# A two-layer hybrid block: RMS root applied after the up projection, attention chains spread over more weight units, convolution taps on GpSimd

## The chip, the cores and the metric

The kernel runs on one core of a Trainium2 chip. The metric is the device time of one execution in microseconds. The kernel before takes 2891.14 us (median of three runs, 2889.9 to 2891.33). The span is the part of an execution that the profile records.

## The reference, cut to what matters

Two transformer-like layers on 256 tokens of width 2048, all float32. What the change touches:

```python
# layer 1
h = rmsnorm(x, g_mix) @ w_in
z, xbc, dt, q, k, v, qi, ki, wi = _split(h, IN_SIZES)
xbc = silu(causal_dwconv(xbc, conv_w, conv_b))          # 4 taps, 1536 channels
y = ssd_chunked(...)                                     # Mamba-2 mixer
y = (y + d_skip * xs) * silu(z)
y_ssd = groupwise_rmsnorm(y, 2 groups) * g_ssd
y_att = dsa_attention(q, k, v, qi, ki, wi)               # 8 heads, top-64 keys
x = x + concat([y_ssd, y_att]) @ w_out
u = rmsnorm(x, g_mlp) @ w_up                             # 2048 -> 8192
x = x + square(relu(u)) @ w_down                         # 8192 -> 2048
# layer 2
proj = rms_norm(x, ln1_w) @ w_in
o_a = nsa_attention(nsa_q, nsa_kv, nsa_gate, ...)
qkv = silu(causal_depthwise_conv(gdn_qkv, conv_w))       # 4 taps, 3072 channels
o_b = gated_deltanet(qkv, gdn_z, ...)
x = x + (g_a * (o_a @ w_pa) + g_b * (o_b @ w_pb)) @ w_o
h = rms_norm(x, ln2_w)
x = x + square(relu(h @ w_up)) @ w_down
```

rmsnorm divides each token's row by its root mean square and multiplies each channel by a gain. Since the divisor is one number per token, `rmsnorm(x, g) @ w` equals `((x*g) @ w) / root`, token by token.

## The kernel before, in words

Activations lie transposed: 128 channels on the partitions, 256 tokens along the free dimension; such a 128x256 piece is a tile, two side by side are a pair. Every big product is float32-exact by splitting: `hi` is the value rounded to the fast type fp32r, `lo` the rest, and TensorE adds hi·hi, hi·lo and lo·hi. So weights and activations both exist as hi and lo.

Weights stream from HBM by SyncE into a ring of four 1 MB pieces (`ring`). Half a piece is a unit (128x1024, eight k-tiles). For each unit ScalarE casts `w_hi` (L1732) and VectorE subtracts `w_lo` (L1036); four such units are held, and ScalarE casts unit n+4 only when TensorE has used unit n. `split_to(unit + UNITS)` issues these two in each engine's program. A column of an output tile takes two units where k is 2048, and TensorE calls L441 (hi weights against hi and lo activations, 512 wide) and L444 (lo weights, 256 wide).

The order of the work is written out by hand. Each engine has its own program made of Python generators. `drain(a, b, project(...))` advances all of them in turn, one step each, and calls that a round; one round holds one weight unit of the projection. `rounds(n)` in a side chain lets n units pass before its next step. The number of rounds must be matched between the engines' programs, since an engine takes its instructions strictly in order: what waits on a semaphore holds all that is behind it.

The places that the change touches:

- `attention(c)`, two chains c = 0 and 1 of three steps sets each, run beside the 24 units of the xbc projection: TensorE logits (L614), VectorE mask, maximum, reciprocal, scale (L1230 to L1237), ScalarE exponentials (L1897), TensorE transposes (L622), ScalarE copy, TensorE output (L633). Both chains do each step in the same round.
- `conv` (L1249 to L1269) evacuates an xbc or GDN tile on VectorE and then computes the four taps there: one L1259 or L1262 and three L1265 per tile, 12 tiles of xbc and 24 of GDN, in all 144 instructions. ScalarE's silu (L1916) of tile t-1 follows after it has lifted tile t.
- `ssd_prepare`, `ssd_output`, `ssd_gate` are the Mamba mixer, beside the z projection and the attention half of the output projection. `ssd_gate` squares the gated output per group (L1969), TensorE sums it over the partitions with a matrix of ones (L705), ScalarE takes the root (L1972), VectorE scales. Group 1 follows group 0 with the same buffers and bank.
- `gathered_norm`, `norm`, `column_pair` start an MLP. The squares of x are taken during the product before (`project_gathered`, L1799, added on GpSimd, L2275); then TensorE sums them (L522 to L526), ScalarE takes the root (L1782), VectorE the reciprocal (L1088), and for each of eight pairs VectorE multiplies by gain and root (L1095), ScalarE casts `h_hi` (L1786), VectorE subtracts `h_lo` (L1099). `column_pair` (L435, L436) computes two output tiles together and waits for each pair of h.
- In the MLP itself `up_tile` and `squared_relu` bring a tile of u from the bank (L1738 and L1056 are the lift and the add of the two halves), then max(u,0)·u in one instruction (L1369), ScalarE's cast (L1995) and VectorE's rest (L1372).

## Time and profile before

| | us |
|---|---|
| median of three runs | 2891.14 |
| the profiled execution, its own time | 2889.39 |
| its span | 2887.2 |
| TensorE busy | 2743.2 (95%) |
| VectorE busy | 1869.5 (65%) |
| ScalarE busy | 1311.0 (45%) |
| GpSimd busy | 35.5 (1%) |

The stages in the order of time, in us from the span's start, as the instructions' lines place them in the timeline: attention chains and xbc from 208 to 305, mixer and z from 308, the output projection until 478, first MLP norm until 505, first MLP body until about 1209, the first half of GDN projections with NSA attention from about 1372 to 1485, the second half with the delta rule from about 1541 to 1648, second MLP norm from 2145 to 2170, second MLP body until 2868. In the MLP bodies TensorE is busy without a gap; its idle time lies between them.

### The profile page before, as it was taken

The numbers are of one execution on the slowest core, as the hardware profiler recorded it, in microseconds if no ns is written. First come the engines' busy times: TensorE is split into PE (matmuls) and PEld (weight loads), VectorE is DVE, ScalarE is ACT, GpSimd is POOL, SyncE is SP. The second block draws the span as 40 slices with busy tenths as digits, with TensorE's granted clock in tenths as the row PEclk, the third lists the DMA queues.
The fourth block names the chain that finished last, engine by engine and source line by source line (L and its number), as shares of the span: only waits on it lengthen the run. The fifth ranks groups of instructions, "written<-read, shape, count | busy, mean of one in ns | idle before, by whom it ended". The sixth has DMA issues, their size and how long they took to land. (4 is left out here: it accounts for less than half of the span.)

```text
span 2887.2 us, 38158 instructions
## 1 busy us (share of the span) xinstructions
PE 2743.2 (95%) x15614; PEld 2366.2 (82%) x15614; DVE 1869.5 (65%) x2582; ACT 1311.0 (45%) x1805; POOL 35.5 (1%) x36
## 2 busy tenths in 40 slices
PE   7998998999999999999898989999989999999998
PEld 6777877888888888788676868878878888888887
DVE  5687687666656666665667767666666666566665
ACT  4545544434434344355554444444434444343443
POOL 0000001000000000100000000000000000000000
PEclk9999999999999999999999999999999999999999
DMA  5344434555555555556232323345445555555553
GB/s 215 134 178 140 152 132 146 190 195 185 192 187 191 190 188 190 208 190 231 102 105 90 122 81 117 132 169 184 173 161 185 189 187 189 186 187 192 188 191 116
DMA packets 66422, 482.05 MB, mean 167 GB/s; under 512 B 7400, under 2 KB 7528, under 8 KB 9033
## 3 DMA queue, kind: packets, MB, share of 16 engines
q1 hardware_dynamic: 64944, 468.74, 46.9%
q0 software_dynamic: 928, 9.70, 0.9%
q8 instruction: 124, 2.03, 0.3%
q10 hardware_dynamic: 376, 1.17, 0.1%
q14 instruction: 50, 0.40, 0.0%
HBM read 473.30 MB, written 6.29 MB: 166 GB/s over the span
## 5 line engine op out<-in xcount | busy, mean ns | idle before, releaser
L1036 DVE TENSOR_TENSOR w_lo<-weight_ring,w_hi 128x1024 fp32r<-128x1024 f32 x886 | 1079.8, 1231 | 592.7 <-ACT w_hi L1732 590.8
L441 PE MATMUL bank<-h,w_hi 128*128 128x512 f32 x4144 | 1333.4, 403 | 4.3 <-DVE h L1702 4.3
L1732 ACT CAST w_hi<-weight_ring 128x1024 fp32r<-128x1024 f32 x886 | 916.7, 1048 | 619.7 <-PE bank L444 602.1
L444 PEld LDWEIGHTS bank<-h,w_lo 128*128 128x128 f32 x4144 | 786.4, 190 | 186.6
L444 PE MATMUL bank<-h,w_lo 128*128 128x256 f32 x4144 | 822.0, 280 | 0.0
L441 PE MATMUL bank<-mix,w_hi 128*128 128x512 f32 x2560 | 808.3, 397 | 6.6 <-DVE w_lo L1036 6.6
L441 PEld LDWEIGHTS bank<-h,w_hi 128*128 128x128 f32 x4144 | 641.7, 191 | 23.3 <-issue 20.0
L444 PEld LDWEIGHTS bank<-mix,w_lo 128*128 128x128 f32 x2560 | 481.9, 188 | 113.8
L444 PE MATMUL bank<-mix,w_lo 128*128 128x256 f32 x2560 | 504.0, 278 | 0.0
L441 PEld LDWEIGHTS bank<-mix,w_hi 128*128 128x128 f32 x2560 | 391.3, 189 | 8.1 <-issue 7.8
L1738 ACT COPY arena<-bank 128x256 f32<-128x256 f32 x283 | 104.6, 371 | 393.4 <-PE bank L444 390.8
L1056 DVE TENSOR_TENSOR arena<-arena,bank 128x256 f32<-128x256 f32 x281 | 117.8, 420 | 161.1 <-ACT arena L1738 160.6
L1106 DVE TENSOR_TENSOR arena<-arena,bank 128x256 f32<-128x256 f32 x176 | 73.9, 420 | 63.2 <-PE bank L444 63.1
L435 PE MATMUL bank<-h,w_hi 128*128 128x512 f32 x128 | 56.4, 468 | 32.8 <-DVE h L1099 32.8
L1109 DVE TENSOR_TENSOR arena<-arena,bank 128x256 f32<-128x256 f32 x176 | 74.1, 421 | 6.0
L1995 ACT CAST mix<-arena 128x512 fp32r<-128x512 f32 x64 | 39.7, 620 | 82.9 <-DVE arena L1369 82.9
L1372 DVE TENSOR_TENSOR mix<-arena,mix 128x512 fp32r<-128x512 f32 x64 | 44.4, 693 | 43.9 <-ACT mix L1995 43.9
L435 PEld LDWEIGHTS bank<-h,w_hi 128*128 128x128 f32 x128 | 28.4, 222 | 46.0 <-DVE h L1099 22.3
L1799 ACT ACTIVATE arena<-arena 128x512 f32<-128x512 f32 x32 | 20.2, 632 | 95.6 <-DVE arena L1109 72.6
L1265 DVE SCALAR_TENSOR_TENSOR arena<-arena,vecs 128x255 f32<-128x255 f32 (+2 forms) x108 | 52.2, 483 | 3.9
L2275 POOL TENSOR_TENSOR arena<-arena 128x512 f32<-128x512 f32 x24 | 31.2, 1302 | 1839.2 <-ACT arena L1799 1839.2
L1369 DVE SCALAR_TENSOR_TENSOR arena<-arena 128x512 f32<-128x512 f32 x64 | 44.3, 692 | 6.7
(318 smaller groups left out, 1496.9 us busy)
## 6 DMA issues: line engine op xcount, KB each, us to landing
weight_ring<-in_w_up SPq DMA_DIRECT2D x128, 1024.0 KB, 4.9
weight_ring<-in_w_down SPq DMA_DIRECT2D x128, 1024.0 KB, 4.9
weight_ring<-in_w_merge SPq DMA_DIRECT2D x32, 1024.0 KB, 4.8
weight_ring<-in_w_gdn SPq DMA_DIRECT2D x24, 1024.0 KB, 4.9
weight_ring<-in_w_papb SPq DMA_DIRECT2D x16, 1024.0 KB, 4.9
...
```

What stands on the lines that cost most here:

```text
L435: e.matmul(bank[:, :], hi, x[:, :, at:at + S], start=first, stop=False)
L441: e.matmul(bank[:, :], w_hi[:, unit_at % UNITS, o + j * P:o + (j + 1) * P], x[:, :, at + j * S:at + (j + 1) * S], start=first and j == 0, ...
L444: done = e.matmul(bank[:, 0:S], w_lo[:, unit_at % UNITS, o + j * P:o + (j + 1) * P], x[:, 0, at + j * S:at + (j + 1) * S], start=False, st ...
L1036: e.tensor_tensor(w_lo[:, i, :], ring[:, p % PIECES, half * UNIT:(half + 1) * UNIT], w_hi[:, i, :].bitcast(F32), ALU.subtract).then_inc(un ...
L1056: e.tensor_tensor(dst, dst, bank[:, 0:S], ALU.add).then_inc(read, 1)
L1106: e.tensor_tensor(tile(xT, t), tile(xT, t), bank[:, 0:S], ALU.add).then_inc(res_half, 1)
L1109: e.tensor_tensor(tile(xT, t), tile(xT, t), bank[:, S:2 * S], ALU.add).then_inc(read, 1)
L1265: e.scalar_tensor_tensor(out=a[:, back:S], in0=src[:, 0:S - back], scalar=vec(name, (3 - back) * tiles + t), in1=a[:, back:S], op0=ALU.mul ...
L1369: e.scalar_tensor_tensor(out=buf, in0=buf, scalar=0.0, in1=buf, op0=ALU.max, op1=ALU.mult).then_inc(up_squared, 1)
L1372: e.tensor_tensor(pair(mix_lo, n_up % 8), buf, pair(mix_hi, n_up % 8).bitcast(F32), ALU.subtract).then_inc(up_lo, 1)
L1732: e.copy(w_hi[:, i, :], ring[:, p % PIECES, half * UNIT:(half + 1) * UNIT]).then_inc(unit_hi, 1)
L1738: e.copy(dst, psum[use % 3][0:dst.shape[0], S:2 * S]).then_inc(lifted, 1)
```

## The change

**MLP norms.** The product x·gain, without the root, is now what the MLP multiplies. During the product before (`project_gathered`, `gained_residual`), each finished tile of x is multiplied by the gain, on ScalarE as hi and on VectorE as lo (`gained`). `column_pair` starts on it, `gathered_norm` comes behind it on TensorE, and the root is awaited in the first `relu_scaled`. There max(u,0) is multiplied by 1/root (one VectorE instruction), ScalarE squares, casts, and VectorE's `lo` of a pair is issued one tile later. The first MLP reads `hn` and writes `mix`; the second reads `mix` and writes `hn`. The norms before the first mixer and before layer 2's projections keep their form.

**First mixer.** Chain 1 of the attention starts three rounds after chain 0; the transposes come three rounds behind the logits, and an iteration has six rounds as before. `ssd_prepare` starts three rounds later on all three engines. `ssd_gate` has its own buffers and banks for its two groups, so all four squares come before the first root.

**Convolutions.** VectorE only evacuates the tile. GpSimd computes the taps: a product, then three times a product into a buffer and a sum, seven instructions per tile, each waiting for the one before it, 252 in all. The DMA that brings x back for the residual is behind the 12 xbc tiles in GpSimd's queue.

```diff
@@ -599,6 +602,7 @@
 
             def attention(c):
                 A = ATT
+                yield from rounds(3 * c)
...
@@ -614,7 +618,7 @@
                         done = e.matmul(bank[0][:, j * nk:(j + 1) * nk], tile(qT, h)[:, qb * P:(qb + 1) * P],
                                         tile(kT, h // 2)[:, 0:nk], start=True, stop=True)
                     done.then_inc(att_pe[c], 1)
-                    yield from rounds(2)
+                    yield from rounds(3)
...
-                    yield from rounds(2)
+                    yield
 
...
             def ssd_prepare():
                 A = PREP
+                yield from rounds(3)
                 e.wait_ge(conv_silu_done, 12)
...
             def ssd_gate():
+                A = GATE["act"]
+                yield from rounds(2)
                 for g in range(2):
-                    yield
-                    if g == 1:
-                        e.wait_ge(gate_act, GATE["act"]["root"])
                     for j in range(2):
-                        e.wait_ge(gate_act, 5 * g + GATE["act"][f"sq{j}"])
-                        e.matmul(psum[7][:, 0:S], ones[:, :], ysq[j][:, 0:S], start=j == 0, stop=False)
-                        done = e.matmul(psum[7][:, 0:S], ones[:, :], ysq[j][:, S:2 * S], start=False, stop=j == 1)
+                        e.wait_ge(gate_act, A[f"sq{g}{j}"])
+                        e.matmul(psum[6 + g][:, 0:S], ones[:, :], ysq[g][j][:, 0:S], start=j == 0, stop=False)
+                        done = e.matmul(psum[6 + g][:, 0:S], ones[:, :], ysq[g][j][:, S:2 * S], start=False, stop=j == 1)
                     done.then_inc(gate_pe, 1)
                     yield
 
...
+            def mlp(n, x, hid):
+
+                ready = xg_lo, [16 * n + k - k % 2 + 2 for k in range(KD)]
                 for f in range(FF // D):
                     if f == 0:
-                        column_pair(hn, normed(i))
-                        drain(project(KD - 2, hn))
+                        column_pair(x, ready)
+                        gathered_norm(1 + 2 * n)
+                        drain(project(KD - 2, x))
                     else:
-                        drain(project(KD, hn))
-                    drain(project(KD, mix, 0, KD, (up_lo, [8 * (4 * n + f) + k // 2 + 1 for k in range(KD)])))
-
-            mlp(1)
+                        drain(project(KD, x))
+                    drain(project(KD, hid, 0, KD, (up_lo, [8 * (4 * n + f) + k // 2 + 1 for k in range(KD)])))
+
+            mlp(0, hn, mix)
...
                 V, A = ATT["dve"], ATT["act"]
                 pr, st = relu_buf[c], (st0, st1)[c]
+                yield from rounds(3 * c + 1)
                 e.wait_ge(score_added, 4 * QI_T)
...
                     e.tensor_reduce(st[:, 0:nh], split(pr, nh), AX_X, ALU.max, negate=True).then_inc(att_dve[c], 1)
+                    yield
                     e.wait_ge(att_act[c], 3 * it + A["exp"])
...
+            n_xg = 0
+
+            def gained(t, gain, dst):
+
+                nonlocal n_xg
+                e.wait_ge(xg_hi, n_xg + 1)
+                e.scalar_tensor_tensor(out=tile(dst[:, 1, :], t), in0=tile(xT, t), scalar=vec(gain, t),
+                                       in1=tile(dst[:, 0, :], t).bitcast(F32), op0=ALU.mult,
+                                       op1=ALU.subtract).then_inc(xg_lo, 1)
+                n_xg += 1
+
+            def gained_residual(gain, dst):
+                def evacuate(t, bank, read):
+                    residual(t, bank, read)
+                    if t > 0:
+                        gained(t - 1, gain, dst)
+                    if t == KD - 1:
+                        gained(t, gain, dst)
                 return evacuate
 
-            drain(attention(0), attention(1), project(12, 2, conv(xbcT, "conv_w", XBC_T, conv_acc_1, 0, "conv_b")))
+            drain(attention(0), attention(1), project(12, 2, to_tiles(xbcT)))
...
+                    if n_up % 32 == 0:
+                        e.wait_ge(norm_root, 2 + 2 * (n_up // 32))
+                        e.reciprocal(root_m, root_m).then_inc(norm_rstd, 1)
+                        e.wait_ge(norm_rstd, 2 + 2 * (n_up // 32))
+                    e.scalar_tensor_tensor(out=split(buf, 2), in0=split(buf, 2), scalar=0.0, in1=over(root_m, 2), op0=ALU.max,
+                                           op1=ALU.mult).then_inc(up_scaled, 1)
                     n_up += 1
                 use += 1
 
+            def up_tiles(first, hid):
                 nonlocal unit
-                for t in range(n):
+                for t in range(first, KD):
                     for i in range(2):
                         split_to(unit + UNITS)
                         unit += 1
                         if i == 1:
-                            squared_relu(t)
+                            relu_scaled(t)
+                            if t % 2 == 0 and t > 0:
+                                squared_lo(n_up - 1, hid)
+                            elif t == KD - 1:
+                                squared_lo(n_up - 1, hid)
                         yield
 
             def mlp(...):
-                split_to(unit + UNITS)
-                norm(i, gain, sq_m, root_m, root_m)
...
+            def project_gathered(per_use, gain=None, dst=None):
+
                 nonlocal unit, use, n_gathered
+
+                def finish(t, at_use):
+                    bank_done(e, at_use)
+                    if gain:
+                        e.activation(tile(dst[:, 0, :], t), tile(xT, t), ACT.Copy, scale=vec(gain, t)).then_inc(xg_hi, 1)
+                    if t % 2:
+                        gather(t // 2, at_use)
+
                 for t in range(KD):
                     for i in range(per_use):
                         split_to(unit + UNITS)
                         unit += 1
                         if i == per_use - 1:
-                            if t % 2:
-                                bank_done(e, use - 1)
-                                gather(t // 2, use)
+                            if t > 0:
+                                finish(t - 1, use - 1)
+                            if t == KD - 1:
+                                finish(t, use)
                             use += 1
                         yield
                 n_gathered += 1
...
-                    e.wait_ge(conv_taps, 4 * (n_conv + 1))
+                    e.wait_ge(conv_taps, 7 * (n_conv + 1))
...
+                    if n_up % 32 == 0:
+                        e.wait_ge(norm_summed, 9 + 2 * (n_up // 32))
+                        e.activation(root_m, psum[7][:, 0:S], ACT.Sqrt, bias=eps[:, 0:1], scale=1.0 / D).then_inc(norm_root, 1)
+                    e.wait_ge(up_scaled, n_up + 1)
+                    e.activation(buf, buf, ACT.Square).then_inc(up_squared, 1)
                     e.wait_ge(up_squared, n_up + 1)
-                    e.copy(pair(mix_hi, n_up % 8), buf).then_inc(up_hi, 1)
+                    e.copy(pair(hid[:, 0, :], n_up % 8), buf).then_inc(up_hi, 1)
...
+            def conv(stage, dst, name, tiles, acc, t_buf, first, with_bias=None):
+
+                nonlocal n_conv, n_tap
+                for i in range(12):
+                    t, src, a = first + i, tile(dst, i), acc[:, (i % 2) * S:(i % 2 + 1) * S]
+                    bank_done(e, USE[stage] + i)
+                    if n_conv >= 2:
+                        e.wait_ge(conv_silu_done, n_conv - 1)
+                    if with_bias:
+                        e.tensor_scalar(a, src, vec(name, 3 * tiles + t), vec(with_bias, t), ALU.mult,
+                                        ALU.add).then_inc(conv_taps, 1)
+                    else:
+                        e.tensor_scalar(a, src, vec(name, 3 * tiles + t), None, ALU.mult).then_inc(conv_taps, 1)
+                    n_tap += 1
+                    for back in (1, 2, 3):
+                        e.wait_ge(conv_taps, n_tap)
+                        e.tensor_scalar(t_buf[:, back:S], src[:, 0:S - back], vec(name, (3 - back) * tiles + t), None,
+                                        ALU.mult).then_inc(conv_taps, 1)
+                        e.wait_ge(conv_taps, n_tap + 1)
+                        e.tensor_tensor(a[:, back:S], a[:, back:S], t_buf[:, back:S], ALU.add).then_inc(conv_taps, 1)
+                        n_tap += 2
+                    n_conv += 1
+
             e.wait_ge(rows_copied, NSA_HEADS)
             e.dma_start(bias_rows, rows).then_inc(rows_written, 16)
+            e.wait_ge(vecs_loaded, 16)
+            conv("xbc", xbcT, "conv_w", XBC_T, conv_acc_1, sq0, 0, "conv_b")
...
+            for half in range(2):
+                conv(f"gdn{half}", gdn_in[half], "conv_w2", 24, conv_acc_g[half], (sqc, arena[:, 1536:2048])[half],
+                     12 * half)
```

Three places show how the instructions move. The first is VectorE in the first GDN half, where an NSA iteration meets a projected tile. Before, from the tile's evacuation (L1056) through chain 0's into chain 1's softmax (L1541 to L1552):

```order
L1056 TENSOR_TENSOR arena<-arena,bank 128x256
L1262 TENSOR_SCALAR arena<-arena,vecs 128x256
L1265 SCALAR_TENSOR_TENSOR arena<-arena,vecs 128x255
L1265 SCALAR_TENSOR_TENSOR arena<-arena,vecs 128x254
L1265 SCALAR_TENSOR_TENSOR arena<-arena,vecs 128x253
L1541 SCALAR_TENSOR_TENSOR arena<-bank,arena 128x256
L1545 TENSOR_REDUCE arena<-arena 128x2
L1547 RECIPROCAL arena<-arena 128x2
L1549 TENSOR_TENSOR arena<-arena 128x2
L1552 TENSOR_TENSOR arena<-arena 128x256
L1541 SCALAR_TENSOR_TENSOR arena<-bank,arena 128x256
```

Now (L1060 is the evacuation, L1553 to L1564 the softmax):

```order
L1060 TENSOR_TENSOR arena<-arena,bank 128x256
L1553 SCALAR_TENSOR_TENSOR arena<-bank,arena 128x256
L1557 TENSOR_REDUCE arena<-arena 128x2
L1559 RECIPROCAL arena<-arena 128x2
L1561 TENSOR_TENSOR arena<-arena 128x2
L1564 TENSOR_TENSOR arena<-arena 128x256
L1553 SCALAR_TENSOR_TENSOR arena<-bank,arena 128x256
```

The four tap instructions between the evacuation and the softmax are gone from VectorE.

The second is VectorE at the start of the attention chains, behind the end of the top-k selection (L1194, L1196). Before, chain 0 (L1230 to L1237), chain 1, then two weight units (L1036) and the first conv tile:

```order
L1194 TENSOR_SCALAR arena<-arena 128x256
L1196 TENSOR_TENSOR arena<-arena,const_mats 128x128
L1230 SCALAR_TENSOR_TENSOR arena<-bank,arena 128x512
L1233 TENSOR_REDUCE arena<-arena 128x4
L1235 RECIPROCAL arena<-arena 128x4
L1237 TENSOR_TENSOR arena<-arena 128x512
L1230 SCALAR_TENSOR_TENSOR arena<-bank,arena 128x512
L1233 TENSOR_REDUCE arena<-arena 128x4
L1235 RECIPROCAL arena<-arena 128x4
L1237 TENSOR_TENSOR arena<-arena 128x512
L1036 TENSOR_TENSOR w_lo<-weight_ring,w_hi 128x1024 x2
L1056 TENSOR_TENSOR arena<-arena,bank 128x256
```

Now (L1235 to L1243 is chain 0, L1040 a weight unit, L1060 an evacuated tile, L1198 and L1200 the selection's end):

```order
L1040 TENSOR_TENSOR w_lo<-weight_ring,w_hi 128x1024
L1235 SCALAR_TENSOR_TENSOR arena<-bank,arena 128x512
L1238 TENSOR_REDUCE arena<-arena 128x4
L1040 TENSOR_TENSOR w_lo<-weight_ring,w_hi 128x1024
L1060 TENSOR_TENSOR arena<-arena,bank 128x256
L1241 RECIPROCAL arena<-arena 128x4
L1243 TENSOR_TENSOR arena<-arena 128x512
L1040 TENSOR_TENSOR w_lo<-weight_ring,w_hi 128x1024 x2
L1060 TENSOR_TENSOR arena<-arena,bank 128x256
L1235 SCALAR_TENSOR_TENSOR arena<-bank,arena 128x512
```

A unit and an evacuation now stand between chain 0's maximum and its reciprocal, and chain 1 comes behind two more units instead of in front of them.

The third is TensorE at the start of the second MLP. Before, the last w_o products, the sums of squares (L522 to L526), then the column pair on h:

```order
L441 MATMUL bank<-h,w_hi 128x512 x2
L444 MATMUL bank<-h,w_lo 128x256 x2
L522 MATMUL bank<-arena,ones 128x256
L523 MATMUL bank<-arena,ones 128x256
L525 MATMUL bank<-arena,ones 128x256
L526 MATMUL bank<-arena,ones 128x256
L435 MATMUL bank<-h,w_hi 128x512
L436 MATMUL bank<-h,w_lo 128x256
L435 MATMUL bank<-h,w_hi 128x512
```

Now the last products of the column pair (L438, L439, 64 rows of them straight behind the w_o products), the sums (L525 to L529), then the next column:

```order
L438 MATMUL bank<-mix,w_hi 128x512
L439 MATMUL bank<-mix,w_lo 128x256
L438 MATMUL bank<-mix,w_hi 128x512
L439 MATMUL bank<-mix,w_lo 128x256
L525 MATMUL bank<-arena,ones 128x256
L526 MATMUL bank<-arena,ones 128x256
L528 MATMUL bank<-arena,ones 128x256
L529 MATMUL bank<-arena,ones 128x256
L444 MATMUL bank<-mix,w_hi 128x512 x2
```

The sums moved from in front of the column pair to behind it, and the pair reads `mix`, not a normed h.

## Rows read from the trace of the kernel before

**Rows 1.** the page, part 1: busy time and share of the span by engine

```profile
PE 2743.2 (95%) x15614; PEld 2366.2 (82%) x15614; DVE 1869.5 (65%) x2582; ACT 1311.0 (45%) x1805; POOL 35.5 (1%) x36
```

**Rows 2.** TensorE's waits over the span: total us, times, longest us

```profile
PE bank L435 <- DVE h L1099: 32.8, 20, 8.6
...
PE bank L870 <- DVE arena L1552: 11.9, 8, 2.4
PE bank L622 <- DVE arena L1237: 10.6, 4, 3.5
...
PE bank L883 <- DVE arena L1555: 8.1, 5, 1.8
...
PE bank L705 <- ACT arena L1969: 5.4, 2, 4.4
```

**Rows 3.** busy time by stretch: span, us busy (instructions) per engine, granted clock, DMA

```profile
792.00:864.00 72.00, 72.00 (x416) 62.86 (x415) 41.45 (x50) 27.12 (x28) 0.00 (x0) 1.00 0.56 190
...
222.50:308.00 85.50, 76.84 (x436) 67.49 (x436) 67.23 (x108) 47.87 (x82) 0.54 (x1) 0.94 0.49 173
...
1372.00:1490.00 118.00, 98.35 (x549) 83.03 (x548) 81.01 (x168) 63.35 (x130) 0.00 (x0) 0.96 0.30 100
...
1545.00:1655.00 110.00, 99.64 (x629) 89.01 (x628) 87.55 (x164) 47.66 (x83) 0.00 (x0) 0.95 0.33 115
```

**Rows 4.** timeline at the two MLP norms: start us, us, instruction, idle before

```profile
478.42 0.60 PE L522 MATMUL bank<-arena,ones 128*128 128x256 f32 x2
...
505.07 0.70 PE L441 MATMUL bank<-h,w_hi 128*128 128x512 f32 x2
...
2144.73 0.59 PE L522 MATMUL bank<-arena,ones 128*128 128x256 f32 x2
...
2147.47 1.28 ACT L1782 ACT_TABLE_LOAD   x1
...
2149.27 1.75 DVE L1088 RECIPROCAL arena<-arena 128x256 f32<-128x256 f32 x1 [0.56 <-ACT arena L1782]
...
2170.13 0.70 PE L441 MATMUL bank<-h,w_hi 128*128 128x512 f32 x2
```

**Rows 5.** timeline of the attention chains and the mixer's start

```profile
219.51 1.11 PE L622 MATMUL bank<-const_mats,arena 128*128 128x128 f32 x4 [3.46 <-DVE arena L1237]
...
308.12 1.12 PE L648 MATMUL bank<-const_mats,arena 128*128 128x128 f32 x4 [3.51 <-ACT arena L1916]
```

**Rows 6.** timeline in the first GDN half's projections

```profile
1392.12 1.52 DVE L1265 SCALAR_TENSOR_TENSOR arena<-arena,vecs 128x255 f32<-128x255 f32 x3
...
1403.90 0.68 PE L883 MATMUL bank<-arena 128*128 128x128 f32 x4 [1.69 <-DVE arena L1555]
...
1484.71 0.42 ACT L1916 ACTIVATE arena<-arena 128x256 f32<-128x256 f32 x1 [1.90 <-DVE arena L1265]
```

**Rows 7.** GpSimd's instructions by line, and a timeline beside VectorE

```profile
L2275 POOL TENSOR_TENSOR arena<-arena 128x512 f32<-128x512 f32 x24 | 31.2, 1302 | 1839.2 <-ACT arena L1799 1839.2
...
L2266 POOL MEMSET ones<- 128x128 f32 x1 | 0.2, 204 | 0.3 <-POOLq L2418 0.3
...
476.31 1.30 POOL L2275 TENSOR_TENSOR arena<-arena 128x512 f32<-128x512 f32 x1 [4.58 <-ACT arena L1799]
...
477.21 1.49 DVE L1036 TENSOR_TENSOR w_lo<-weight_ring,w_hi 128x1024 fp32r<-128x1024 f32 x1 [1.69 <-ACT w_hi L1732]
```

**Rows 8.** the page, part 5: count, busy us and mean ns of one

```profile
L1036 DVE TENSOR_TENSOR w_lo<-weight_ring,w_hi 128x1024 fp32r<-128x1024 f32 x886 | 1079.8, 1231 | 592.7 <-ACT w_hi L1732 590.8
...
L1732 ACT CAST w_hi<-weight_ring 128x1024 fp32r<-128x1024 f32 x886 | 916.7, 1048 | 619.7 <-PE bank L444 602.1
...
L1106 DVE TENSOR_TENSOR arena<-arena,bank 128x256 f32<-128x256 f32 x176 | 73.9, 420 | 63.2 <-PE bank L444 63.1
...
L1799 ACT ACTIVATE arena<-arena 128x512 f32<-128x512 f32 x32 | 20.2, 632 | 95.6 <-DVE arena L1109 72.6
...
L1369 DVE SCALAR_TENSOR_TENSOR arena<-arena 128x512 f32<-128x512 f32 x64 | 44.3, 692 | 6.7
```

158 lines of the change are left out of this document (66 added, 92 removed).

## The prediction

> **What bounds the kernel now.** I read the busy times first. TensorE is busy for 95% of the span [rows 1], so only its idle time and its slow time are to be had: 2887.2 - 2743.2 = 144 us idle. Then the stretches [rows 3]: in an MLP body (792 to 864) it is busy for all 72 us at a granted clock of 1.00, with 416 matmuls, 0.173 us each. A weight unit of 16 matmuls so takes 2.8 us, a column of two units 5.5, a column pair 11.1. In the three other stretches it is idle for 9, 20 and 10 us, and the mean granted clock is 0.94 to 0.96: part of the time it runs at the lower of its levels, 1.2 GHz instead of 2.4. A mean of 0.95 over 100 us costs about 5 us more. The waits then say for whom it waits [rows 2]: VectorE's normed h 32.8 us, the NSA chains 11.9 and 8.1, the attention chains 10.6, the gate's squares 5.4. The timelines show each place [rows 4 to 6].
>
> **The two MLP norms.** From the first sum of squares to the first column behind the pair, 505.07 - 478.42 = 26.65 us pass at the first MLP and 2170.13 - 2144.73 = 25.40 at the second [rows 4]. Of it the pair itself is 11.1 us of work and the four sums about 1.7 (a line of two records shows 0.6). These 12.8 stay. The gain products that replace the norm are ready long before the pair needs the last of them: it asks for tiles 14 and 15 after 14/16 of 11.1 = 9.7 us, and these need two more instructions on VectorE and ScalarE behind the last residual. So 13.8 and 12.6 us go, and what is late next is the root. Behind the pair stand, in order: two lifts on ScalarE (0.9 us), the root with its table load (1.8 from load to reciprocal), the reciprocal 1.75 [rows 4], the scaled relu 0.69, the square 0.63 and a cast of the same size [rows 8]: 6.5 us, and only then ScalarE casts the next weight unit (1.05) and VectorE subtracts (1.23) [rows 8]. That is 8.8 us. TensorE has the sums and two units in hand, 1.7 + 5.6 = 7.3. I charge 1.5 us at the second MLP and 1.1 at the first, where the gate has left the root's table in place. Gain: 12.7 + 11.1 = 23.8 us; the least is 18, if each first root costs 3 us more.
>
> In the MLP bodies 64 squares move to ScalarE, 64 x 0.63 = 40 us, which is busy for 27.1 us of 72 there [rows 3]; I count them at nothing. The last pair's chain to `lo` grows from about 2.8 to 3.8 us, and the down product asks for it 14/16 of a column, 4.9 us, after its start. If that cover of 1.1 us were gone, each of the eight changes from up to down would cost.
>
> The gain products add 16 x 2 instructions in each product before. In the first one a unit takes 2.9 us and VectorE has 1.23 + 2 x 0.42 [rows 8] + about 0.44 = 2.5 us per unit. It fits, with 0.4 to spare.
>
> **Attention chains.** Before, the first transposes waited 3.46 us [rows 5] and all four long ones 10.6 [rows 2]. The stretch loses about 4 us more to the clock. Afterwards chain 0 has three units before its transposes. The first of them still waits: TensorE arrived at 216.05 and will arrive 2.8 us later less half of the logits, near 217.9. VectorE comes from the top-k selection, was done at 219.5 and has one weight unit more in front (1.23), so 220.7. That leaves 2.8 us of wait and about 1.8 of slow clock. The later ones have 8.4 us for a chain of about 4 and go. I take 9 us of gain, between 4 and 13.
>
> **The mixer's start.** It waited 3.51 us for the last silu [rows 5], and then ran slow, some 2.3 us. Three units of cover (8.4 us) replace that. But ScalarE and VectorE both still stand until the last tile's convolution is done, and then have 2.3 us of work for the fourth unit ahead. The limit is a convolution that ends 5.9 us after the tile. I take 1.3 us of stall, a gain of 4.5; between -2 and +6.
>
> **The gate.** 5.4 us of waits for squares go [rows 2]. But VectorE's reciprocals, scalings and rests for both groups now have three units less until the out_ssd column needs them: 2 x (1.75 + 4 x 0.42 + 2 x 0.69) = 9.6 us, with units and residuals of 2.1 between them, against 2.9 per unit on TensorE. I work out a new wait of about 6 us for `lo` of group 1. So nothing is gained, between -4 and +5.
>
> **The convolutions.** VectorE gives up four instructions per tile: 36 tiles, three of them 1.52 us together [rows 6], with the first 1.9. GpSimd's price is not in the trace. Its 512-wide sum takes 1.30 us; a memset of 128 columns 0.20 [rows 7]. For a sum of 255 columns that bounds 0.65 to 1.30, for a product 0.3 to 1.30. I take 0.72 and 0.45, near halved length plus a fixed part: 3 x 0.72 + 4 x 0.45 = 4.0, and six waits of 0.1: 4.6 us per tile. The bounds are 3.2 and 9.1.
>
> VectorE and GpSimd also meet. A w_lo subtraction that started 0.4 us before the end of GpSimd's sum took 1.49 us instead of 1.23 [rows 7, 8]. So each collision costs a wait, on one of the two. Per xbc tile VectorE has two such subtractions, 2.5 us. Were all of it serial, the convolution would take 4.6 + 2.5 = 7.1 us, against a tile every 5.6 in the last five xbc tiles and about 8 to 10 elsewhere.
>
> The Trainium skill speaks against this part: "GPSIMD Engine Reference", § 4.1 Engine selection, advises against elementwise work there, two-input operations at about half VectorE's speed, and "SBUF — State Buffer", § SBUF: two separate sides, says that the shared port pair is an exclusive lock held for a whole instruction. The trace shows the collision, though the subtraction of 1.49 us ended sooner than a lock to the sum's very end would allow (1.63). By such a lock all 2.5 us are serial, towards the first rival. By the first page's 2.6 cycles per element a sum would be about 0.55 us plus its dispatch, and a tile about 4 us, as an estimate.
>
> What it gives: in the first GDN half the wait of 1.69 us at L883 stood behind the taps in VectorE's queue, and the chain in front of L870 began 1.9 us late for the same reason [rows 6, 2]. Both go. The stretch 1372 to 1490 is 20 us idle and loses about 4 by its clock [rows 3]. I leave 3 us of short waits, 3 of collisions and 3.5 at the end, where ScalarE waited 1.90 us for the last taps [rows 6] and will wait about 5. Gain 14.5, between 3 and 22. In the second half (1545 to 1655) 10 us are idle and 5 slow [rows 3], and the delta rule's chains are mostly their own length. Gain 5, between -3 and 10.
>
> **Sum.** 23.8 + 9 + 4.5 + 0 + 14.5 + 5 = 56.8. From the profiled execution's 2889.39 this gives 2832.6. The median is 1.75 us above that execution: 2834.
>
> **The rivals.**
>
> *GpSimd sets the pace in part.* If a tile takes 8 us, which needs each of the seven instructions to wait about 0.5 us for VectorE, the last five xbc tiles fall behind by 4 x 2.4 = 9.7 us and the last silu comes 18.6 us after its tile, 12.7 beyond the limit. The GDN halves give back 7 and 4, as ScalarE is held inside the chains. 24 us less: 2858. For it: VectorE's two-input work fills 2.5 us of each 5.6. Against: GpSimd's own work is half of 8 us.
>
> *VectorE, not TensorE, bounds the output projection.* The gain products come onto an engine that is behind after the gate. If the new wait there is 10 us and the pair starts with VectorE 4 us late, the sum loses 8 to 10: 2843.
>
> *Slower than before.* GpSimd paces all 36 tiles. The three stretches hold them now in about 96 + 118 + 110 = 324 us, 9.0 a tile. With the 24 us from the norms, the sign turns at 348/36 = 9.7 us per tile; at 12 us the kernel takes 2891 + 36 x 12 - 348 = 2975. It needs instructions at their upper bound (9.1 us) and collisions on top. Against it: the memset row.
>
> **How the numbers follow.** The forecast has 0.60, with its own range 2820 to 2848. GpSimd's partial pace 0.20, the output projection 0.12, slower 0.03; 0.05 is left for more gain than I count, to 2815, since the lost time of these stretches is more than what I book. The range that holds it 8 times in 10 is 2818 to 2862. A measurement can tell 0.2%, 6 us, from no change. Faster 0.96, same 0.01, slower 0.03.
>
> **What would show it.** In the profile after: the first MLP column (L435 before) straight behind the product, and 14 to 16 us from the end of the product to the second column, instead of 25 to 27; GpSimd's tile in 4 to 6 us; the waits of the transposes L622 down to one of about 3 us; no wait at L883 for VectorE's copy; a new wait of the out_ssd column for the gate's `lo`. Wrong would be a wait of TensorE for w_lo in the xbc columns, a silu held for more than 6 us, or gaps in the MLP bodies.

## The result and the profile after

The changed kernel takes 2864.04 us, median of 4 runs (2862.56 to 2865.05), against 2891.23 (2889.90 to 2891.82) for the kernel before on the same chip. The ratio is 0.9906 with a 95% interval of 0.9889 to 0.9923. It is faster by 27 us, less than half of the 57 that were forecast, and 2 us outside the range. The profiled execution has a span of 2860.6 us.

Both kernels issue the same 6832 column matmuls by `w_hi` in the same order (L435 and L441 before, L438 and L444 after), so the n-th of them stands for the same piece of work. Start before minus start after is then a gain that can be followed through the program. The table gives what it grows by from one mark to the next. At each mark it is a mean over 17 neighbouring matmuls, because single ones jump where a chain's instructions fall on the other side of them. Before the first mark it is 0.5 us.

| stretch (matmul n, start before) | forecast | measured |
|---|---|---|
| xbc, attention, state preparation and output (8 to 736, to 400.8 us) | 9 + 4.5 | -1.0 |
| gate and output projection (to 920, 475.7 us) | 0 | -2.2 |
| first MLP norm (to 984, 513.6 us) | 12.7 | 11.6 |
| MLP body, NSA preparation (to 3272, 1374.9 us) | 0 | 0.0 |
| first GDN half (to 3500, 1515.2 us) | 14.5 | 3.6 |
| second GDN half (to 3760, 1693.4 us) | 5 | 3.8 |
| merges (to 4600, 2080.7 us) | 0 | -0.5 |
| second MLP norm (to 4850, 2182.1 us) | 11.1 | 10.9 |
| rest | 0 | 0.0 |

The norms came out as forecast. What is missing, 14.5 us in the first mixer and 12.1 in the GDN halves, lies where GpSimd now computes the taps. The small terms are 2.2 at the gate and output projection, 1.3 at the norms and 0.5 in the merges.

TensorE's busy time on the page, to be held against [rows 1], and its waits (who waits, for whom: total us, times, longest us), against [rows 2]:

```profile
PE 2734.1 (96%) x15614; PEld 2362.7 (83%) x15614; DVE 1782.8 (62%) x2422; ACT 1360.9 (48%) x1889; POOL 291.7 (10%) x288
```

```profile
PE bank L438 <- DVE h L1103: 17.3, 9, 8.9
...
PE bank L874 <- DVE arena L1564: 10.7, 8, 2.0
...
PE bank L887 <- ACT arena L2171: 9.8, 3, 6.4
PE bank L626 <- DVE arena L1243: 8.7, 4, 4.9
...
PE bank L444 <- DVE mix L1352: 5.7, 2, 5.3
...
PE bank L653 <- ACT arena L1938: 5.0, 1, 5.0
...
PE bank L946 <- ACT arena L2213: 3.5, 1, 3.5
...
PE bank L637 <- ACT arena L1925: 3.1, 3, 1.8
```

L435's 32.8 us are down to L438's 17.3, which are the norms before the first mixer and before layer 2's projections; the change leaves them. The gate's own waits (L705) went, and the wait that was forecast for the out_ssd column came (5.3 for `mix` L1352). But the softmax transposes of the NSA chains (L874) wait nearly as before, L887 no longer waits for VectorE and instead for ScalarE's copy, up to 6.4 us, the mixer's start (L653) waits 5.0 instead of 3.5, and L637 and L946 wait for ScalarE where they had not.

The stretches that answer to [rows 3], with the same columns; the first is MLP work, the last two begin and end with the same matmuls as there, to within 1.5 us:

```profile
783.00:855.00 72.00, 72.00 (x416) 62.80 (x415) 41.56 (x51) 26.98 (x28) 0.00 (x0) 1.00 0.55 190
222.50:308.00 85.50, 78.57 (x456) 68.29 (x455) 45.32 (x59) 51.62 (x88) 75.57 (x74) 0.98 0.38 127
1363.00:1477.50 114.50, 97.56 (x555) 83.06 (x554) 63.88 (x121) 63.92 (x130) 79.92 (x84) 0.95 0.32 111
1532.00:1637.00 105.00, 96.24 (x631) 87.40 (x630) 70.90 (x118) 48.36 (x84) 81.00 (x83) 0.96 0.32 111
```

In the xbc stretch, the second line, VectorE's busy time fell from 67.2 to 45.3 us, and GpSimd is busy 75.6 of 85.5: the work was moved onto an engine that is now nearly full. In the first GDN half TensorE still idles 17 us, for 20 before, and its granted clock is no better.

GpSimd's instructions in the changed kernel, by line (min/median/max duration in ns):

```profile
L2317 POOL TENSOR_SCALAR arena<-arena,vecs x108: 925/935/2832, 224.7 to 1630.7; 128x255 f32<-128x255 f32 x36, 128x254 f32<-128x254 f32 x36, 128x253 f32<-128x253 f32 x36
L2320 POOL TENSOR_TENSOR arena<-arena x108: 717/735/1767, 225.7 to 1631.8; 128x255 f32<-128x255 f32 x36, 128x254 f32<-128x254 f32 x36, 128x253 f32<-128x253 f32 x36
...
L2313 POOL TENSOR_SCALAR arena<-arena,vecs x24: 923/932/2007, 1364.4 to 1626.0; 128x256 f32<-128x256 f32 x24
L2310 POOL TENSOR_SCALAR arena<-arena,vecs x12: 544/554/3145, 221.4 to 310.9; 128x256 f32<-128x256 f32 x12
```

The sum takes 0.735 us where 0.72 was forecast. The product (L2317, and L2313 as a GDN tile's first tap) takes 0.93, where 0.45 was. L2310, a product and the bias in one instruction, takes only 0.55. So an undisturbed GDN tile is 4 x 0.93 + 3 x 0.73 and six gaps of 0.09, 6.4 us instead of 4.6 (an xbc tile 6.05, its first instruction being L2310). Most tiles are disturbed: from the first product's start to the last sum's end they take 7.5 us in the mean of the 36, since the products and sums that meet a subtraction of VectorE take longer (mean of L2317 1.09 us, of L2320 0.90).

Timelines of GpSimd, of ScalarE and of TensorE at the last tile of the first GDN half (start us, us, instruction, idle before):

```profile
1461.01 0.93 POOL L2313 TENSOR_SCALAR arena<-arena,vecs 128x256 f32<-128x256 f32 x1 [3.85 <-DVE arena L1060]
...
1466.72 0.72 POOL L2320 TENSOR_TENSOR arena<-arena 128x253 f32<-128x253 f32 x1
```

```profile
1467.47 0.42 ACT L1938 ACTIVATE arena<-arena 128x256 f32<-128x256 f32 x1 [6.40 <-POOL arena L2320]
```

```profile
1468.41 2.08 PE L887 MATMUL bank<-arena 128*128 128x128 f32 x8 [6.42 <-ACT arena L2171]
```

GpSimd runs the seven instructions without a disturbance, ScalarE stands 6.40 us at the silu, and the copy that TensorE's L887 waits for is queued behind it. At the same mark of the kernel before, ScalarE stood 1.90 us [rows 6]. The same shows over the whole program: ScalarE's waits at a silu were 6.5 us in 3 times before (L1916), and are now

```profile
ACT arena L1938 <- POOL arena L2320: 61.6, 25, 6.4
```

At the first MLP norm, against [rows 4], the timeline of TensorE (the sums' start, the first column behind the pair, the column after it):

```profile
493.10 0.59 PE L525 MATMUL bank<-arena,ones 128*128 128x256 f32 x2
...
494.63 0.81 PE L444 MATMUL bank<-h,w_hi 128*128 128x512 f32 x2
...
501.77 0.70 PE L444 MATMUL bank<-h,w_hi 128*128 128x512 f32 x2 [1.21 <-DVE w_lo L1040]
```

The sums of squares now stand behind the column pair, the next column follows them without a wait, and what is left to wait is 1.21 us one column later, for a `w_lo` that VectorE subtracts behind the reciprocal; the forecast had 1.1. At the second norm it is 1.51, forecast 1.5.

### The profile page after: what moved, and what is told of

Same layout as the page of the kernel before. It is cut to its first block and busy times, and to the rows that moved or that the text cites. A ratio compares the mean times of both kernels' runs of the same rounds, so it can differ in the third digit from the quotient of the medians.

```text
span 2860.6 us, 38328 instructions
## 1 busy us (share of the span) xinstructions
PE 2734.1 (96%) x15614; PEld 2362.7 (83%) x15614; DVE 1782.8 (62%) x2422; ACT 1360.9 (48%) x1889; POOL 291.7 (10%) x288
## 5 line engine op out<-in xcount | busy, mean ns | idle before, releaser
L1040 DVE TENSOR_TENSOR w_lo<-weight_ring,w_hi 128x1024 fp32r<-128x1024 f32 x886 | 1078.9, 1228 | 715.7 <-ACT w_hi L1744 714.8
L444 PE MATMUL bank<-h,w_hi 128*128 128x512 f32 x4176 | 1340.9, 403 | 6.6 <-DVE h L1714 4.3
L444 PE MATMUL bank<-mix,w_hi 128*128 128x512 f32 x2528 | 801.2, 398 | 13.8 <-DVE w_lo L1040 8.1
L444 PEld LDWEIGHTS bank<-h,w_hi 128*128 128x128 f32 x4176 | 644.6, 191 | 25.9 <-issue 20.7
L444 PEld LDWEIGHTS bank<-mix,w_hi 128*128 128x128 f32 x2528 | 387.7, 190 | 16.0 <-issue 10.1
L2297 POOL TENSOR_TENSOR arena<-arena 128x512 f32<-128x512 f32 x24 | 38.8, 1616 | 1782.1 <-ACT arena L1811 1782.1
L1060 DVE TENSOR_TENSOR arena<-arena,bank 128x256 f32<-128x256 f32 x281 | 117.3, 419 | 146.1 <-ACT arena L1750 145.5
L2317 POOL TENSOR_SCALAR arena<-arena,vecs 128x255 f32<-128x255 f32 (+2 forms) x108 | 117.5, 1088 | 10.5
L2320 POOL TENSOR_TENSOR arena<-arena 128x255 f32<-128x255 f32 (+2 forms) x108 | 96.8, 896 | 9.0
L2019 ACT ACTIVATE arena<-arena 128x512 f32<-128x512 f32 x64 | 40.5, 633 | 85.0 <-DVE arena L1378 85.0
L438 PE MATMUL bank<-h,w_hi 128*128 128x512 f32 x96 | 40.4, 453 | 17.3 <-DVE h L1103 17.3
L2313 POOL TENSOR_SCALAR arena<-arena,vecs 128x256 f32<-128x256 f32 x24 | 24.5, 1020 | 253.8 <-DVE arena L1060 253.8
L1938 ACT ACTIVATE arena<-arena 128x256 f32<-128x256 f32 x36 | 15.0, 418 | 61.7 <-POOL arena L2320 61.6
```

The source lines that it names most:

```text
L444: e.matmul(bank[:, :], w_hi[:, unit_at % UNITS, o + j * P:o + (j + 1) * P], x[:, :, at + j * S:at + (j + 1) * S], start=first and j == 0, ...
L1040: e.tensor_tensor(w_lo[:, i, :], ring[:, p % PIECES, half * UNIT:(half + 1) * UNIT], w_hi[:, i, :].bitcast(F32), ALU.subtract).then_inc(un ...
L1060: e.tensor_tensor(dst, dst, bank[:, 0:S], ALU.add).then_inc(read, 1)
L2019: e.activation(buf, buf, ACT.Square).then_inc(up_squared, 1)
L2317: e.tensor_scalar(t_buf[:, back:S], src[:, 0:S - back], vec(name, (3 - back) * tiles + t), None, ALU.mult).then_inc(conv_taps, 1)
L2320: e.tensor_tensor(a[:, back:S], a[:, back:S], t_buf[:, back:S], ALU.add).then_inc(conv_taps, 1)
```

## The experiments

Two theories stood first. **A**: GpSimd's tile is dearer than forecast and its silus stand in ScalarE's queue ahead of what the chains need. **B**: the attention and mixer-start edits are worth nothing in themselves. Those two are called the spacing below. D, the price of the tile alone, and others are told at their runs. The last columns are gains over the kernel before by matched matmuls, as in the table above. Each comes from one profiled execution.

| run | median us | ratio to before (95%) | first mixer | GDN 1 | GDN 2 |
|---|---|---|---|---|---|
| changed kernel | 2864.0 | 0.9906 (0.9889 to 0.9923) | -1.0 | 3.6 | 3.8 |
| mlp_only | 2870.3 | 0.9930 (0.9915 to 0.9944) | 0.2 | 0.4 | -0.2 |
| v_all | 2868.5 | 0.9927 (0.9911 to 0.9944) | 1.0 | 0.2 | 0.0 |
| v_xbc | 2860.6 | 0.9897 (0.9882 to 0.9912) | 0.6 | 3.6 | 3.8 |
| late_silu | 2848.1 | 0.9852 (0.9837 to 0.9866) | -0.9 | 12.3 | 9.1 |
| late_both | 2844.9 | 0.9836 (0.9818 to 0.9853) | 1.4 | 12.6 | 9.0 |
| xbc_v_late | 2843.4 | 0.9831 (0.9814 to 0.9848) | 0.9 | 14.1 | 10.1 |
| late_old_gate | 2845.8 | 0.9838 (0.9818 to 0.9858) | -1.1 | 14.2 | 10.0 |
| late_old_att | 2858.1 | 0.9882 (0.9865 to 0.9899) | -13.9 | 14.1 | 10.0 |
| three_products | 2832.1 | 0.9796 (0.9782 to 0.9811) | 12.3 | 14.1 | 10.0 |
| two_op | 2837.3 | 0.9816 (0.9800 to 0.9833) | 9.3 | 11.5 | 9.7 |
| two_op_old_att | 2849.7 | 0.9852 (0.9834 to 0.9869) | -3.4 | 11.9 | 8.5 |
| two_op_late_both | 2830.2 | 0.9793 (0.9778 to 0.9807) | 9.2 | 19.5 | 8.7 |
| split_8 | 2832.1 | 0.9799 (0.9784 to 0.9813) | 14.4 | 13.8 | 8.8 |
| two_op_split | 2827.4 | 0.9776 (0.9755 to 0.9797) | 13.5 | 19.5 | 8.6 |

The first MLP norm gives 11.6 to 11.9 and the second 10.7 to 10.9 in every one of them.

The column of the first mixer holds two terms of the forecast, 9 us for the attention chains and 4.5 for the mixer's start. At matmul 536 (301 us in the kernel before) both kernels have finished the attention chains and neither has begun the state preparation, so the column can be parted there:

| run | attention chains | mixer's start, preparation and output |
|---|---|---|
| forecast | 9 | 4.5 |
| changed kernel | 0.1 | -1.1 |
| v_all | -7.7 | 8.6 |
| late_silu | -0.9 | 0.0 |
| late_old_att | -2.7 | -11.2 |
| late_both | 5.6 | -4.1 |
| three_products | 3.8 | 8.5 |
| two_op | 2.4 | 6.9 |
| two_op_old_att | 1.9 | -5.3 |
| split_8 | 5.7 | 8.6 |

### All convolutions back on VectorE: v_all

```
-            drain(attention(0), attention(1), project(12, 2, to_tiles(xbcT)))
+            drain(attention(0), attention(1), project(12, 2, conv(xbcT, "conv_w", XBC_T, conv_acc_1, 0, "conv_b")))
...
-                yield from project(12, 2, to_tiles(gdn_in[half]))
+                yield from project(12, 2, conv(gdn_in[half], "conv_w2", 24, conv_acc_g[half], 12 * half))
```

> The changed kernel with all three convolutions back on VectorE (one scaled copy and three multiply-adds per tile); MLP, chains and gate as in the changed kernel. Theory A (the convolutions on GpSimd hid what the attention and mixer-start edits give, and gave 7 us net in the GDN halves): the MLP edits keep 23, the gate keeps its loss of 3.5, attention and mixer start give 8 to 13, the GDN halves are as in the kernel before; about 2860 us. Theory B (attention and mixer-start edits are worth nothing by themselves): 2871 us.

Measured 2868.5, near B's 2871. The first mixer gains 1.0 us, not 8 to 13, so A's share for the spacing was wrong here. But the 1.0 is not two edits that do nothing: the chains lose 7.7 us and the mixer's start gives 8.6. TensorE's timeline shows what became of it: the two L622 waits at 219.51 and 223.46 us (3.46 [rows 5] and 2.83) turned into a single longer one, and new ones stand at the output matmuls.

```profile
224.13 1.11 PE L626 MATMUL bank<-const_mats,arena 128*128 128x128 f32 x4 [6.92 <-DVE arena L1243]
...
247.13 1.28 PE L637 MATMUL bank<-arena 128*128 128x128 f32 x6 [2.04 <-ACT arena L1949]
```

All waits of L626 and L637 over 0.45 us sum to 17.0 in this stretch, where those of L622 were 10.6 [rows 2]; the wait at the mixer's start (3.51 [rows 5]) is gone. The attention chains' new rounds cost with VectorE loaded, the later start of the preparation pays. The GDN halves are as before, within 0.2: their 7.4 us in the changed kernel are GpSimd's.

### Only the xbc convolution back on VectorE: v_xbc

```
-            conv("xbc", xbcT, "conv_w", XBC_T, conv_acc_1, sq0, 0, "conv_b")
```

(On VectorE as in v_all; the GDN tiles stay on GpSimd.)

> The changed kernel with only the first convolution (twelve xbc tiles) back on VectorE, the 24 GDN tiles stay on GpSimd. Theory A: 7 us under the run with all three on VectorE, some 10 under the changed kernel, 2853 us. Theory B: 2864, no difference from the changed kernel.

Measured 2860.6, between A's 2853 and B's 2864, and 3.4 under the changed kernel; the two ratios' intervals overlap, so the times alone don't show that difference. The GDN halves give exactly what they gave there, 3.6 and 3.8. In the matched work the xbc convolution at GpSimd's real price is a small loss (-1.0 against 0.6).

### The last silu of each GDN half two units later: late_silu

```
-                yield from project(12, 2, gdn_in[half], conv_silu(gdn_in[half], conv_acc_g[half]))
-                yield from project(4, 2, gdn_z[half], silu)
+                last = conv_silu(gdn_in[half], conv_acc_g[half])
+                yield from project(12, 2, gdn_in[half], last, hold=True)
+                z = project(4, 2, gdn_z[half], silu)
+                for _ in range(2):
+                    next(z)
+                    yield
+                last(tile(gdn_in[half], 11), None)
+                yield from z
```

(With `hold`, ScalarE's `project` doesn't issue the silu of its last tile.)

> The changed kernel with one move on ScalarE: the silu of the last tile of each GDN half is issued two units later, behind the copies of the NSA or delta chains, instead of right after the tile before. Theory A (the 6.42 us wait of TensorE at L887 is ScalarE standing at that silu for GpSimd's 6.4 us of products and sums): the wait goes with the slow clock after it, 7 to 11 us in the first half and 0 to 4 in the second, 2852 us. Rival C (the chain behind it is late anyway, or the delta rule waits for the silu instead): under 3 us, 2861 or more.

Measured 2848.1, where A had 2852: one instruction per GDN half, moved on ScalarE, is worth 16 us. The stretch after the wait, by busy time (span, us busy and instructions per engine, granted clock, DMA), first in the changed kernel:

```profile
1461.00:1487.00 26.00, 19.58 (x88) 16.59 (x86) 7.98 (x17) 8.39 (x19) 5.88 (x7) 0.74 0.21 78
```

and the same 26 us in late_silu:

```profile
1461.00:1487.00 26.00, 24.64 (x148) 21.09 (x148) 15.82 (x28) 16.18 (x30) 7.80 (x7) 1.00 0.46 153
```

TensorE's granted clock, 1.00 being its level of 2.4 GHz, is 0.74 over the stretch with the wait of 6.42 us (from 1465.5 to 1479.1 us it is 0.50, that is 1.2 GHz) and 1.00 without the wait, and 88 matmuls stand against 148. By matched matmuls the changed kernel was 23.4 us ahead at matmul 3447 and 12.5 at 3456: a hold of 6.4 us cost 10.9, of which the wait is 6.4 and the rest goes with the slower clock.

### The fourth tap left out on GpSimd: three_products

```
-                    for back in (1, 2, 3):
+                    for back in (1, 2):
```

> The changed kernel with the fourth tap (one product and one sum per tile) left out on GpSimd, so the convolution's output lacks that term. A tile then costs 0.93 x 3 + 0.73 x 2 and gaps, 4.6 us, which is what the forecast took for the whole tile. Theory D (the forecast failed by the price of a tile alone): 2834 to 2840 us. Theory A (the price and the place of the silus in ScalarE's queue both count; the last silu still holds ScalarE 4.7 us): 2850 to 2856.

Measured 2832.1, D's side, and even below it; the forecast was 2834. With an undisturbed GDN tile at 4.6 us the first mixer gives 12.3 (forecast 13.5), the first GDN half 14.1 (14.5) and the second 10.0 (5). The 12.3 is near 13.5 by luck: the chains give 3.8 of the 9 forecast, the mixer's start 8.5 where 4.5 was. A's 2850 fell. The silu at the end of the half still held ScalarE, 4.57 us, and the gain fell from 46.1 to 37.5 between matmuls 3447 and 3456, 8.6 us; but the eleven tiles before it had given more.

### The xbc silus later too: late_both

```
-                yield from project(12, 2, xbcT, conv_silu(xbcT, conv_acc_1))
+                yield from project(12, 2, xbcT, xbc_silu, hold=True, lag=2)
...
+            def project_z():
+                z = project(8, 2, zT, silu)
+                for n in range(2):
+                    next(z)
+                    yield
+                    xbc_silu(tile(xbcT, 10 + n), None)
+                yield from z
```

> late_silu, and in the xbc stretch too the silus one tile further behind (the silu of tile t at tile t + 2, the last two behind the first two z units; VectorE's wait for them goes into the state preparation). Theory P (GpSimd's tile of 6.2 to 8 us costs time only because ScalarE stands at the silus in front of the attention's copies and weight casts): the first mixer gains what leaving out a tap gained there, 8 to 12 us, 2838 us. Theory T (GpSimd's throughput itself is short there): 0 to 3 us, 2846.

Measured 2844.9, T's 2846. P was half right: the waits inside the attention chains shrank (at matmul 470 the gain was 7.2 us, against 2.1 in late_silu), and then two thirds of what the chains had gained over late_silu was paid at the mixer's start:

```profile
317.31 1.12 PE L653 MATMUL bank<-const_mats,arena 128*128 128x128 f32 x4 [10.30 <-ACT arena L1938]
```

GpSimd is behind there, whatever ScalarE does meanwhile: VectorE delivers the last tiles at 281.29, 287.11, 293.58 and 299.41 us, about every 6 us, and they cost GpSimd 6.1 undisturbed and 7.0 to 7.8 as they ran. It ends the last one at 316.8.

### late_silu with xbc on VectorE, the old gate, the old spacing: xbc_v_late, late_old_gate, late_old_att

The first is v_xbc with late_silu's edit, the other two put these back into late_silu:

```
-                yield from rounds(2)
                 for g in range(2):
+                    yield
+                    if g == 1:
+                        e.wait_ge(gate_act, GATE["act"]["root"])
```

```
                 A = ATT
-                yield from rounds(3 * c)
...
                 A = PREP
-                yield from rounds(3)
                 e.wait_ge(conv_silu_done, 12)
```

(with the rest of the gate, and of the attention's and preparation's rounds, on all engines as in the kernel before)

> late_silu with the xbc convolution on VectorE. The two differences should add, since they lie in different stretches: 2848.1 less the 3.4 us that v_xbc is under the changed kernel, 2844.7 us. If the xbc convolution on GpSimd with its taps left whole is no loss, 2848.

Measured 2843.4 for 2844.7: the totals add, the parts only in part. Of the 5 us under late_silu the first mixer gives 1.8; 2.8 lie in the GDN halves (14.1 and 10.1 against 12.3 and 9.1), where the two programs are the same. late_old_gate and late_old_att below have 14 and 10 there too, late_both has the lower pair; why is open.

> late_silu with the gate as in the kernel before (groups one after the other, one root at a time, one bank). The matched work lost 2.1 us over the gate in the changed kernel; theory G (the new wait for the rests of group 1 costs more than the waits that went): 2846 us. If the loss there comes from the convolution's backlog and not from the gate's order: 2848 or more.

Measured 2845.8, G's number, but not for G's reason. Over the gate the matched work loses 1.3 us with the old order and 1.6 with the new. The rest of the difference lies in the GDN halves (14.2 and 10.0 against 12.3 and 9.1), where the two programs are the same. Of the loss at the gate about 1 us is there with everything but the MLP as before (mlp_only, -1.0). The waits there are the old ones (1.04 and 4.38 us), but the granted clock in 400 to 425 us was 0.86 instead of 0.93, and why is open.

> late_silu with the attention rounds and the start of the state preparation as in the kernel before (the convolutions still on GpSimd). Theory B (the wider spacing is worth nothing while VectorE and ScalarE carry this load): within 2 us of 2848. If the spacing gives the 9 + 4.5 us of the forecast once VectorE is free: 2855 to 2862.

Measured 2858.1: B fell for this surrounding, as to the mixer's start. TensorE's timeline, at the start of the preparation:

```profile
322.61 1.11 PE L651 MATMUL bank<-const_mats,arena 128*128 128x128 f32 x4 [15.11 <-ACT arena L1933]
```

Without the spacing the start waits 15.1 us for GpSimd. Together the two edits are worth 13 us with a GpSimd that is behind (-0.9 against -13.9), and 1 us (v_all against mlp_only) with VectorE. The later start of the preparation gives 11.2 of the 13; the chains' rounds give 1.8.

### The product in another form: two_op

```
-                        e.tensor_scalar(t_buf[:, back:S], src[:, 0:S - back], vec(name, (3 - back) * tiles + t), None,
-                                        ALU.mult).then_inc(conv_taps, 1)
+                        e.tensor_scalar(t_buf[:, back:S], src[:, 0:S - back], vec(name, (3 - back) * tiles + t), 0.0,
+                                        ALU.mult, ALU.add).then_inc(conv_taps, 1)
```

(and the first GDN tap in the same way)

> The changed kernel with each GpSimd product written as a product and an added 0.0 in one instruction, like the first tap of an xbc tile (which adds the bias: 0.55 us for 256 columns, where the plain product of the first GDN tap took 0.93 for the same 256). Nothing is left out. Theory D (the forecast failed by the price of the product; at 4.6 us per tile its terms were right): if the form sets the 0.93, a tile costs 4 x 0.55 + 3 x 0.73 and gaps, 4.9 us, and the time falls nearly to that of the run without the fourth tap, 2832 to 2842 us. Rival E (0.93 comes from the operands' place or length, or the form with a constant is no faster): 0.93 stays and the time is 2864.

Measured 2837.3, all taps computed. The same lines of GpSimd as above:

```profile
L2317 POOL TENSOR_SCALAR arena<-arena,vecs x108: 482/495/2392, 225.5 to 1608.6; 128x255 f32<-128x255 f32 x36, 128x254 f32<-128x254 f32 x36, 128x253 f32<-128x253 f32 x36
...
L2313 POOL TENSOR_SCALAR arena<-arena,vecs x24: 482/482/1558, 1353.4 to 1604.9; 128x256 f32<-128x256 f32 x24
```

The product with an added 0.0 takes 0.49 us, the bare product 0.93, on the same operands. E fell. Why the bare form is slower no run shows. An undisturbed GDN tile is now 4.65 us, from 1444.20 to 1448.85 in the timeline, and that is the forecast's tile; the mean of all 36, with what the meetings with VectorE cost, fell from 7.5 to 5.8. ScalarE's waits at silus are 27.6 us in 16 times.

### The cheap form with the other edits: two_op_late_both, split_8, two_op_old_att, two_op_split

split_8 is late_both with xbc tiles 8 to 11 on VectorE:

```
+                    if i < 8:
+                        add_half(tile(dst, i), bank, read)
+                        return
```

> The product-and-add form together with the later silus of late_both. If the form is cheap, GpSimd's backlog at the start of the state preparation (10.3 us of wait in late_both) goes too, and the time is 2822 to 2832; if 0.93 stays, 2845 as late_both.

Measured 2830.2, in the range. The first GDN half gives 19.5, as neither price nor place holds ScalarE; the first mixer no more than two_op's.

> late_both with the last four of the twelve xbc tiles convolved on VectorE, products as in the changed kernel. Theory T (the start of the state preparation waits for GpSimd's throughput, a backlog of the last tiles): the 10.3 us go and 7 are kept of it, 2836 us. If VectorE's four tiles cost the attention chains the same, 2843 or more.

Measured 2832.1 for 2836. The 10.30 us at the start are gone and the first mixer gives 14.4, so it was GpSimd's backlog that stood there, as T says.

> two_op (the changed kernel with the cheap form of the product) with the attention rounds and the start of the state preparation as in the kernel before. Open is which part of the first mixer's 9.3 us gain in two_op the spacing gives. Theory S (the forecast's 9 + 4.5 us are the spacing's, once VectorE has no convolutions and GpSimd keeps pace): 2846 to 2851 us. Theory F (VectorE being free gives it, the spacing is worth nothing): 2837 to 2840.

Measured 2849.7, S's number: the spacing is worth 12.7 us (9.3 against -3.4). That this is near the forecast's 13.5 is a coincidence. Without the spacing TensorE's timeline has at the start of the preparation

```profile
311.65 1.11 PE L651 MATMUL bank<-const_mats,arena 128*128 128x128 f32 x4 [9.49 <-ACT arena L1933]
```

where the kernel before waited 3.51 [rows 5]: even with the cheap product GpSimd is behind there. The later start of the preparation takes this wait away and is worth 12.2 (6.9 against -5.3). The chains' wider rounds, which the forecast had at 9, are worth 0.5 (2.4 against 1.9).

> split_8 with the cheap form of the product. The parts lie in different stretches and should add: the first mixer as in split_8 (14 us gained), the GDN halves as in two_op_late_both (19 + 9), 2824 us. If the xbc tiles on VectorE cost more than the backlog of a tile of 5 us does: 2829 or more.

Measured 2827.4, 3 above the expected 2824. The first mixer gives 13.5, the halves 19.5 and 8.6. It is the fastest of all, 1.3% under the changed kernel by the two ratios.

### The MLP edits alone: mlp_only

```
-            drain(attention(0), attention(1), project(12, 2, to_tiles(xbcT)))
+            drain(attention(0), attention(1), project(12, 2, conv(xbcT, "conv_w", XBC_T, conv_acc_1, 0, "conv_b")))
```

(with the spacing, the gate and the GDN convolutions as in the kernel before too)

> Only the MLP edits: attention rounds, mixer start, gate and all convolutions as in the kernel before. Theory B (the other edits are worth nothing without GpSimd): within 3 us of the 2868.5 of the run with all convolutions on VectorE, that is 2866 to 2870. If the chains' edits do gain 9 there, 2877.

Measured 2870.3. The MLP edits alone are 20 us. The chains' and gate's edits without GpSimd add 1.8, which the two intervals can't tell from nothing: B, in this surrounding, as a sum of a loss in the chains and a gain at the mixer's start.

## Why the prediction was wrong, step by step

- **The MLP norms** (12.7 + 11.1): measured 11.6 + 10.9, with stalls of 1.21 and 1.51 for the 1.1 and 1.5 worked out. Right, mechanism and size (22.5 of 23.8).
- **Attention chains and mixer start** (9 + 4.5): measured 0.1 and -1.1. With GpSimd's tile at 4.6 us they give 12.3 with the fourth tap left out, and 9.3 with all taps in the cheap form. So the price is what took the sum, but the two terms are wrong by themselves and cancel: the chains give 3.8 and 2.4, less than the least of 4 that was allowed, the start 8.5 and 6.9, more than the most of 6. "The later ones have 8.4 us for a chain of about 4 and go" failed: waits of 0.95 to 1.85 us stay in two_op, the wider rounds themselves are worth 0.5 to 1.8 us, and with the taps on VectorE the chains lose 7.7. The first wait, 2.8 us in the forecast, was 4.9 in every run that has GpSimd on all twelve tiles or on eight, and the spacing.
- **The gate** (0, between -4 and +5): the new wait for group 1's `lo` came, 5.28 us where 6 was worked out, and the stretch lost 2.2. Inside the bounds.
- **GpSimd's tile** (4.6 us): this is the step that failed and set the time. "0.72 for a sum" was right (0.73), "0.45 for a product" was half of the truth (0.93), and four products per GDN tile make 1.9 us. The value was taken from near the memset's row [rows 7] and "half length plus a fixed part" of a sum; 0.93 lay well inside the bounds of 0.3 to 1.30, and the tile's 6.4 within 3.2 to 9.1. As they ran, the tiles took 7.5, outside the "4 to 6 us" named as the sign; 1.7 of the 2.9 too much go with the product's form (5.8 in two_op), the rest with the meetings with VectorE. But the rival with 8 us per tile got only 24 us of loss (2858), and the range ended 4 us above it, when a tile of 7.5 lost 30. Put at 4.6 undisturbed by two different edits, the kernel takes 2832 and 2837 us, against a forecast of 2834. That the total comes so close is partly luck: the terms above and below miss by up to 6 us each, in both directions.
- **First GDN half** (14.5): measured 3.6. Up to matmul 3447 it was 14.4 us of gain (8.9 to 23.4), then the last silu took 10.9 back. "3.5 at the end, where ScalarE will wait about 5": ScalarE waited 6.40, and the wait of 6.42 on TensorE cost 10.9 with the slow clock that went with it. Even at the forecast price that end cost 8.6, so 3.5 was wrong by itself, which more gain in the tiles before made up for.
- **Second GDN half** (5): measured 3.8, but for 9 to 10 with the silu moved or GpSimd cheaper. The size was too small and the price took the difference.
- **Rivals.** "GpSimd sets the pace in part" (2858 at 8 us per tile, chance 0.20) is what happened, at 7.5 us per tile, with the reason only partly as given: the waiting for VectorE is about 1.2 us per tile, not 3.5, and the product's own 0.93 is the larger part. The rival's 18.6 us for the last silu is 0.9 more than its terms, 9.7 and 8. The silu held for more than 6 us was named as a sign, and came. VectorE bounding the output projection did not come.
- **Collisions.** "Each collision costs a wait, on one of the two" holds. The mean of a `w_lo` subtraction is 1.228 us, for 1.231 before [rows 8], so over the program VectorE lost nothing; in the mean it is GpSimd that pays, as in this pair (GpSimd's timeline, then VectorE's):

```profile
258.50 2.00 POOL L2317 TENSOR_SCALAR arena<-arena,vecs 128x253 f32<-128x253 f32 x1
```

```profile
258.48 1.23 DVE L1040 TENSOR_TENSOR w_lo<-weight_ring,w_hi 128x1024 fp32r<-128x1024 f32 x1 [4.54 <-ACT w_hi L1744]
```

The product began 0.02 us after the subtraction and took 2.00 instead of 0.93, so it ended 0.79 us after the subtraction. Fifteen products (L2317) began during a subtraction, and fourteen of them ended 0.79 or 0.80 us after it, the other 1.85. This agrees with the Trainium skill's "SBUF — State Buffer", § SBUF: two separate sides, which has the shared port pair locked for a whole instruction. The 1.49 us of [rows 7] is of the same kind: that subtraction ended 1.09 us after the sum, and so did one in the changed kernel that began 0.04 us after a sum (264.01 us, 1.78 long). In the other order the trace does not agree for the one-input product: a subtraction at 244.51 us, 0.33 after a product of 0.93 began, took its usual 1.23. None of the 14 that began 0.33 us or more behind the start of an L2317 product of that length was held up, so what the Trainium skill says is not borne out for that instruction, and the measurement decides. The same skill's "GPSIMD Engine Reference", § 4.1 Engine selection, has one-input operations at roughly line rate; here the one-input product in its bare form (0.93) was dearer than the two-input sum (0.73), and the measurement decides.
